# Filler products of the token norms in a two-block transformer kernel

## The reference, cut to what matters

```python
def rmsnorm(x, g):
    y = xf * rsqrt(mean(xf * xf, axis=-1, keepdims=True) + NORM_EPS)
    return y * g
# first block, per layer
h = rmsnorm(x, g_pre) * (1 + scale) + shift
x = x + gate * rmsnorm(mixer(h), g_post)
# second block, per layer
h = modulate(rms_norm(x, norm1_g), sh1, sc1)
y = conformer_conv(h, ...)     # layer 0, has a layer_norm inside
y = hgrn2_mixer(h, ...)        # layer 1
x = x + g1 * y
h = modulate(rms_norm(x, norm2_g), sh2, sc2)
x = x + g2 * sq_relu_mlp(h, w1, w2)
# at the end: rms_norm(x, final_g)
```

## The kernel before, in words

| norm | where (us of the span) | busy | followed by |
|---|---|---|---|
| post-norm and wide pre-norm, layer 0 | 346 to 368 | (2,1,3), (1,3,0) | projection of the odd mixer |
| post-norm and wide norm1, layer 1 | 702 to 725 | (2,1,3), (1,3,0) | first projection of the convolution |
| LayerNorm of the convolution | 898 to 910 | (0,2,3) | its second projection |
| norm2, layer 0 | 955 to 963 | (4,1,2) | MLP |
| norm1, layer 1 | 1318 to 1325 | (2,1,2) | projection of the recurrence |
| norm2, layer 1 | 1781 to 1790 | (4,1,2) | MLP |
| last norm | 2144 to 2155 | (2,1,0) | output |

## Time and profile before

### The profile page before, as it was taken

The page is one execution under the profiler, slowest core; times in us unless marked ns, Lnnn a source line. Parts: engine busy times, 40 slices in busy tenths (PEclk is TensorE's granted clock), DMA queues, the critical chain, the costliest instruction groups (busy, mean ns, idle before and its releaser), DMA issues.

```text
span 2157.5 us, 26466 instructions
## 1 busy us (share of the span) xinstructions
PE 2064.9 (96%) x9808; PEld 1588.1 (74%) x9808; DVE 1458.2 (68%) x2639; ACT 921.3 (43%) x1739; POOL 16.0 (1%) x15
## 2 busy tenths in 40 slices
PE   4988899999999999899999999999999899999998
PEld 2765566777667676578888887788888777888886
DVE  7667777667475799876555566998988965343343
ACT  3345554354443532344223234666666644232231
POOL 1000000000000000000000000000000000000000
PEclk8999999999999999999999999999999999999999
DMA  8522222533225111046555552111111122222321
GB/s 338 195 94 90 64 79 69 175 127 130 86 79 166 50 49 49 20 147 202 168 196 183 171 185 77 51 58 49 56 53 50 50 69 81 95 98 98 97 89 59
DMA packets 65982, 228.73 MB, mean 106 GB/s; under 512 B 7104, under 2 KB 9280, under 8 KB 65728
## 3 DMA queue, kind: packets, MB, share of 16 engines
q1 hardware_dynamic: 65856, 227.05, 31.6%
HBM read 224.93 MB, written 2.10 MB: 105 GB/s over the span
## 4 chain that ended last, share of the span: by engine, by line
PE 73%; DVE 17%; ACT 5%; issue 4%; DMA 1%; SPq 1%; DVEq 0%; ACTq 0%
PE bank L379 20%; PE bank L381 19%; PE bank L380 19%; DVE arena L1813 6%; PE bank L2099 3%; DVE w_lo L315 2%; PE bank L1259 1%; PE bank L705 1%; PE bank L1273 1%; PE bank L1284 1%; PE bank L1004 1%; DMA arena<-ada_dram 1%; ACT w_hi L306 1%; ACT arena L1302 1%; DVE arena L2045 1%
## 5 line engine op out<-in xcount | busy, mean ns | idle before, releaser
L379 PE MATMUL bank<-h_hi,w_hi 128*128 128x512 f32 x1540 | 633.2, 411 | 2.9 <-DVE h_lo L2193 0.9
L381 PE MATMUL bank<-h_hi,w_lo 128*128 128x512 f32 x1540 | 606.6, 394 | 0.0
L380 PE MATMUL bank<-h_lo,w_hi 128*128 128x512 f32 x1540 | 604.7, 393 | 0.0
L306 ACT ACTIVATE w_hi<-w_raw 128x1024 fp32r<-128x1024 f32 (+3 forms) x293 | 290.6, 993 | 282.7 <-PE bank L381 269.3
L315 DVE TENSOR_TENSOR w_lo<-w_raw,w_hi 128x1024 fp32r<-128x1024 f32 (+3 forms) x290 | 333.4, 1151 | 74.5 <-ACT w_hi L306 74.2
L379 PEld LDWEIGHTS bank<-h_hi,w_hi 128*128 128x128 f32 x1540 | 292.9, 190 | 69.1 <-issue 6.5
L381 PEld LDWEIGHTS bank<-h_hi,w_lo 128*128 128x128 f32 x1540 | 291.3, 189 | 63.9
L380 PEld LDWEIGHTS bank<-h_lo,w_hi 128*128 128x128 f32 x1540 | 292.7, 190 | 57.2 <-issue 3.9
L379 PE MATMUL bank<-a_hi_t,w_hi 128*128 128x512 f32 x512 | 203.1, 397 | 0.0
L380 PE MATMUL bank<-a_lo_t,w_hi 128*128 128x512 f32 x512 | 203.1, 397 | 0.0
L381 PE MATMUL bank<-a_hi_t,w_lo 128*128 128x512 f32 x512 | 203.0, 397 | 0.0
(11 more groups left out here) (284 smaller groups left out, 2536.8 us busy)
## 6 DMA issues: line engine op xcount, KB each, us to landing
w_raw<-weights_dram SPq DMA_DIRECT2D x261, 512.0 KB, 3.6
ada_raw<-ada_dram SPq DMA_DIRECT2D x128, 512.0 KB, 3.6
arena<-ada_dram SPq DMA_DIRECT2D x8, 1024.0 KB, 15.5
w_raw<-weights_dram SPq DMA_DIRECT2D x16, 256.0 KB, 2.6
xT<-x_dram SPq DMA_DIRECT2D x1, 2048.0 KB, 14.1
out_dram<-xT SPq DMA_DIRECT2D x8, 256.0 KB, 2.2
tables<-tables_dram SPq DMA_DIRECT2D x1, 1536.0 KB, 19.8
w_raw<-weights_dram SPq DMA_DIRECT2D x8, 144.0 KB, 3.5
```

The costliest lines, as they stand in the source:

```text
L306: nc.scalar.activation(WH[:, slot, 0:w], RAW[:, raw, 0:w], ACT.Copy).then_inc(w_hi_ready, 1)
L379: nc.tensor.matmul(o, WH[:, slot, cols], self.hi(k), start=(i == 0), stop=False)
L380: nc.tensor.matmul(o, WH[:, slot, cols], self.lo(k), start=False, stop=False)
L381: last = nc.tensor.matmul(o, WL[:, slot, cols], self.hi(k), start=False, stop=(i == self.K - 1))
```

## The change

Every `busy=...` argument of the nine `TokenNorm`s is taken out. `self.busy` is then None, so that `keep_busy` is called with a count of 0 and the wait for the filler's bank falls away. That is 45 fillers of 512 columns and 16 of 128 columns, 122 MATMUL and 122 LDWEIGHTS records. The filler products of the attention and of the recurrence are other lines of the kernel and stay.

```diff
-            post = TokenNorm(Y, C, ..., out=..., add=..., busy=(7, (2, 1, 3)))
+            post = TokenNorm(Y, C, ..., out=..., add=...)
...
-            return TokenNorm(XT, C, ..., banks=(5,), busy=(7, (1, 3, 0)), wide=True), gains
+            return TokenNorm(XT, C, ..., banks=(5,), wide=True), gains
...
-            post = TokenNorm(Y, C, ..., scratch_kb=68, busy=(7, (2, 1, 3)))
+            post = TokenNorm(Y, C, ..., scratch_kb=68)
...
-            pre, pre_gain = second_norm(0, 0, post.normed, banks=(5,), scratch_kb=68, busy=(7, (1, 3, 0)), wide=True)
+            pre, pre_gain = second_norm(0, 0, post.normed, banks=(5,), scratch_kb=68, wide=True)
...
-                norm, gains = second_norm(1, 0, p2.free, added=7, busy=(7, (2, 1, 2)))
+                norm, gains = second_norm(1, 0, p2.free, added=7)
...
-                norm = TokenNorm(XT, C, lambda k: vec("final", k), p2.free, added=7, out=..., busy=(7, (2, 1, 0)))
+                norm = TokenNorm(XT, C, lambda k: vec("final", k), p2.free, added=7, out=...)
...
-            ln = TokenNorm(Y, C, ..., func=ACT.Silu, centered=True, scratch_kb=40, banks=(6, 7), busy=(3, (0, 2, 3)))
+            ln = TokenNorm(Y, C, ..., func=ACT.Silu, centered=True, scratch_kb=40, banks=(6, 7))
...
-            n2, gains = second_norm(0, 1, pr.free, added=7, busy=(7, (4, 1, 2)))
+            n2, gains = second_norm(0, 1, pr.free, added=7)
...
-            n2, gains = second_norm(1, 1, pr.free, added=7, busy=(7, (4, 1, 2)))
+            n2, gains = second_norm(1, 1, pr.free, added=7)
```

More of the change, by code:

```diff
@@ L1525, in even_layer @@
             y2 = Project(8, 4, P, HH, HL, [], add, evac_engine="dve", chunks=mla_out.done)
-            post = TokenNorm(Y, C, lambda k: GAIN[:, 8 + k:9 + k], y2.free, added=7, out=lambda k: XT[:, k, :], add=lambda k: XT[:, k, :], busy=(7, (2, 1, 3)))
+            post = TokenNorm(Y, C, lambda k: GAIN[:, 8 + k:9 + k], y2.free, added=7, out=lambda k: XT[:, k, :], add=lambda k: XT[:, k, :])
             post_gain = gate_gain(0)
@@ L1535, in odd_norm @@
             gains = mod_gain(1)
-            return TokenNorm(XT, C, lambda k: GAIN[:, k:k + 1], made, hi=HH, lo=HL, bias=lambda k: MOD[:, 24 + k:25 + k], banks=(5,), busy=(7, (1, 3, 0)), wide=True), gains
+            return TokenNorm(XT, C, lambda k: GAIN[:, k:k + 1], made, hi=HH, lo=HL, bias=lambda k: MOD[:, 24 + k:25 + k], banks=(5,), wide=True), gains
         class HeadNorm(Stage):
@@ L1692, in odd_layer @@
                   *((Do(lambda pe, i=i: yp.chunk(pe, i, range(3))), 31.2 + 0.7 * i, 1) for i in range(C - 1)))
-            post = TokenNorm(Y, C, lambda k: GAIN[:, 8 + k:9 + k], yp.free, added=7, out=lambda k: XT[:, k, :], add=lambda k: XT[:, k, :], scratch_kb=68, busy=(7, (2, 1, 3)))
+            post = TokenNorm(Y, C, lambda k: GAIN[:, 8 + k:9 + k], yp.free, added=7, out=lambda k: XT[:, k, :], add=lambda k: XT[:, k, :], scratch_kb=68)
             post_gain = gate_gain(1)
-            pre, pre_gain = second_norm(0, 0, post.normed, banks=(5,), scratch_kb=68, busy=(7, (1, 3, 0)), wide=True)
+            pre, pre_gain = second_norm(0, 0, post.normed, banks=(5,), scratch_kb=68, wide=True)
             weave((yp, 2, 1), (ModBias(44, 48), 2.1, 1), (post_gain, 2.15, 1), (post, 3.2, 0.2, 0, 3), (post, 4.2, 1, 3, 6), (post, 6.9, 1, 6, 7), (post, 8.2, 1, 7, 8), (ModBias(48, 81), 7.2, 1), (pre_gain, 7.3, 1), (post, 8.3, 1, C, C + 1),
@@ L1753, in mlp @@
             if l == 0:
-                norm, gains = second_norm(1, 0, p2.free, added=7, busy=(7, (2, 1, 2)))
+                norm, gains = second_norm(1, 0, p2.free, added=7)
                 weave((p2, 0, 1), (ModBias(96, N_ADA), 4.1, 1), (gains, 4.2, 1), (lower_bounds(), 4.3, 1), (norm, 1.2, 1, 0, 6), (norm, 6.9, 1, 6, 7), (norm, 8.2, 1, 7, 8), (norm, 8.3, 1, 8, 9))
             else:
-                norm = TokenNorm(XT, C, lambda k: vec("final", k), p2.free, added=7, out=lambda k: XT[:, k, :], busy=(7, (2, 1, 0)))
+                norm = TokenNorm(XT, C, lambda k: vec("final", k), p2.free, added=7, out=lambda k: XT[:, k, :])
                 weave((p2, 0, 1), (norm, 1.2, 1, 0, 6), (norm, 6.9, 1, 6, 7), (norm, 8.2, 1, 7, 8), (norm, 8.3, 1, 8, 9), (norm, 9, 1, 9, 18))
@@ L1841, in conv_layer @@
             conv = DepthwiseConv(U, Y, view(56, (2, 15, P)), glu, [9] * 7 + [15])
-            ln = TokenNorm(Y, C, lambda k: vec("ln_g", k), conv.made, hi=HH, lo=HL, bias=lambda k: vec("ln_b", k), func=ACT.Silu, centered=True, scratch_kb=40, banks=(6, 7), busy=(3, (0, 2, 3)))
+            ln = TokenNorm(Y, C, lambda k: vec("ln_g", k), conv.made, hi=HH, lo=HL, bias=lambda k: vec("ln_b", k), func=ACT.Silu, centered=True, scratch_kb=40, banks=(6, 7))
             weave((n1, 0, 0.1, C + 1, 2 * C + 2), (Do(None, None, pad), 1.9, 1), (pc, 2, 1), (conv, 3.3, 1), (ln, 6.4, 2, 0, 8), (ln, 20.5, 1, 8, 9))
             pr = Project(8, C, P, HH, HL, [], residual(48 + 16), evac_engine="dve", chunks=ln.split, ada=ada_next(range(7)), outer=3, early=ln.h_ready)
-            n2, gains = second_norm(0, 1, pr.free, added=7, busy=(7, (4, 1, 2)))
+            n2, gains = second_norm(0, 1, pr.free, added=7)
             weave((ln, 0, 0.1, C + 1, 2 * C + 2), (pr, 2, 1), (n2, 3.2, 0.2, 0, 3), (n2, 4.2, 1, 3, 6), (n2, 6.9, 1, 6, 7), (n2, 8.2, 1, 7, 8), (ModBias(81, 88), 7.2, 1), (gains, 7.3, 1), (n2, 8.3, 1, 8, 9))
```

## The result

Six runs of the changed kernel have a median of 2163.69 us (2162.41 to 2169.58) against 2155.93 us (2153.83 to 2158.21): ratio 1.0039, 95% interval 1.0028 to 1.0049. It is slower, by 7.8 us between the medians, where 9.5 were forecast. The profiled execution took 2162.41 us.

What follows compares the result with a forecast made beforehand. TensorE, with 73% of the chain, was taken to bound the kernel. Losses of 18.0 us from clock falls less gains of 8.5 made it 9.5 slower: median 2155.1 to 2164.6, stated as 2164.5 us, range 2157.5 to 2171.5.

Steps and rivals of the forecast that it cites:

- The gains: In the norms, sums and spreadings no longer held back by fillers: 8.5 us saved, firm to about 1 us.
- E: Norm1 of layer 1: gain 1.0 against loss 2.6, +1.6 us; its sum was to come 0.85 earlier.
- G: The last norm: gain 1.0 against loss 0.4, -0.6 us, since only DVE and the output follow.
- F: Norm2 of layer 1: gain 2.7 against loss 2.6, -0.1 us; its sum was to come 2.55 earlier.
- D: Norm2 of layer 0: gain 1.2 against loss 3.0, +1.8 us; its sum was to come 1.05 earlier.
- A: Layer 0's post- and pre-norm: gain 0.7 against loss 2.9, +2.2 us; the post-norm's sum 0.55 earlier.
- The losses: In every norm the clock falls, slowing the next projection's start, the spreading and rarely the second sum: 18.0 us.
- The spreading's odds: Spreading at half clock, +0.9 us: charged 0.6 in both post-norms and norm2 of layer 0, 0.4 in the others.
- B: Layer 1's post- and pre-norm: gain 0.15 against loss 2.5, +2.35 us.
- The projection at half clock: Start of the projection after a norm: 4.7 us at half clock, costing 2.2 us, or 1.7 into the convolution.
- The LayerNorm: LayerNorm: gain 1.75 from an earlier spreading against loss 4.0, of which 1.8 for its slow spreading; +2.25 us.
- The pre-norms: Slow ones-products catch up before the last sum: costed at nothing, or +0.9 us in each of two if still slow.

Runs made afterwards that it cites:

- e3: Kernel before, each 512-column filler replaced by four one-column products and each 128-column filler by two: 2197.06 us, ratio 1.017.
- e4: Kernel before with the fillers out only in norm2 of layer 1: 2163.48 us, run once.
- e8: Kernel before keeping only fillers after the spreading and the pre-norms' large ones; earlier ones and the pre-norms' small ones out: 2160.52 us.
- e5: The trimmed kernel e1, but with all fillers of layer 0's post-norm back as before: 2152.32 us against 2157.75, ratio 0.9977.
- e6: As e5, also without the single filler ahead of the spreading in six norms: 2151.2 us, ratio 0.9971 against the kernel before.
- e1: Kernel before with one to three fillers fewer in five norms and the LayerNorm, the others kept: 2153.63 us against 2158.24, ratio 0.9972.
- e9: As e6, plus five fillers ahead of the LayerNorm's wait for the convolution's last chunk: 2151.89 us, ratio 0.9979 against the kernel before.

## Why the prediction was right

**The mechanism** was right: the clock falls in every norm, and the new delay is larger than what the late sums give back. e3 shows that it is the full-width fillers that held the clock, since one-column products in their places did not; e4 that it falls in a norm that alone lost its fillers, e8 the separate price at the projection, e5 and e6 that the gains are there once the clock holds. The close number (9.5 forecast, 7.8 between the medians, +8.2 in the norms) owes something to luck: the losses at the projections came out smaller than forecast (9.4 for 12.6 us), those ahead of them larger (7.3 for 5.4, if the gains were as forecast).

**The gains**, 8.5 forecast. In the changed kernel itself the second sum ends earlier after the first by 0.84 in E and G and 2.55 in F, and the LayerNorm's spreading starts 5.16 us after the sums' start instead of 6.98: 1.82 where 1.75 was forecast. With the clock held the gains measure 0.8 to 0.9 in D, E and G and 2.5 in F for the fillers taken away in e5, and 0.6 for the middle ones, where 0.9 was forecast. A's 0.55 was never seen alone, since the clock fell when one filler was taken away, and D's full 1.05 neither.

**The losses**, 18.0 forecast. If the gains were the 8.5 of the forecast, the measured +8.2 leave 16.7, and they were shared out otherwise:
- *The spreading's odds.* I gave 0.6 and 0.4 for a slow spreading. It was slow in A, B, D, E and G (1.98 to 2.08), and mostly fast in F (1.24). So G gave 0.1 instead of 0.6, and F gave 0.4 instead of 0.1. The second sum was slow in D (1.86) and in part in A (1.24). The fall came at different distances from the last dense product, 2.5 us in D and 4.5 in B, so odds were the right form, and the forecast ones were too low here.
- *The projection at half clock.* It was slow for 3.3 us in D and the LayerNorm, 3.4 in A (from 0.6 us on), 4.8 in F, 5.1 in B and 5.8 in E; the mean is 4.3, where 4.7 was forecast. What each stretch takes more behind the projection's first product is 1.4 in A, 1.1 in B, 0.7 in the LayerNorm, 1.4 in D, 2.6 in E and 2.2 in F: 9.4, where 12.6 was forecast. E cost 2.5 instead of 1.6 in full behind that start; its projection starts as far from the first sum as before (7.05 and 7.10 us), since the late sum's gain pays for the slow spreading:

```profile
1325.71 0.77 PE L397 MATMUL bank<-h_hi,w_hi 128*128 128x512 f32 x1 [1.69 <-ACT h_hi L819]
...
1331.91 0.39 PE L379 MATMUL bank<-h_hi,w_hi 128*128 128x512 f32 x1
```

- *The LayerNorm* shows best where the term was mis-sized: 2.2 forecast. Its timeline, beside the earlier trace rows:

```profile
896.50 3.58 PE L739 MATMUL bank<-tables,arena 128*128 128x1 f32 x16 [4.89 <-DVE arena L1817]
901.66 3.55 PE L776 MATMUL bank<-tables,stats 128*128 128x128 f32 x16 [1.59 <-DVE stats L852]
908.36 0.77 PE L397 MATMUL bank<-h_hi,w_hi 128*128 128x512 f32 x1 [3.14 <-ACT arena L817]
...
912.03 0.39 PE L379 MATMUL bank<-h_hi,w_hi 128*128 128x512 f32 x1
```

The spreading took 3.55 as forecast, and the projection starts 11.86 after the sums instead of 12.16. Then nine products take 3.67 us; before they took 2.68, in which 0.37 was a wait for DVE. Of the 1.0 lost, 0.3 was regained at the start and 0.3 behind, where DVE's 2.05 per chunk and TensorE's 2.07 are nearly even: +0.4 in all. I had the two numbers side by side for the convolution's first projection, and not for this one.
- *The pre-norms.* Costed at nothing, rightly: in layer 0 twelve records of ones-products take 7.96 us without a pause, the clock comes back within them, the last two wait for ACT again, and a second fall comes in the projection, after a pause of 3.14:

```profile
346.12 2.08 PE L776 MATMUL bank<-tables,stats 128*128 128x128 f32 x8 [0.57 <-DVE stats L855]
350.52 7.96 PE L760 MATMUL bank<-arena,tables 128*128 128x512 f32 x12 [2.32 <-ACT arena L792]
...
360.67 1.13 PE L760 MATMUL bank<-arena,tables 128*128 128x512 f32 x2 [0.81 <-ACT arena L792]
364.94 0.47 PE L397 MATMUL bank<-h_hi,w_hi 128*128 128x512 f32 x1 [3.14 <-ACT h_hi L819]
365.24 0.39 PE L398 MATMUL bank<-h_hi,w_lo 128*128 128x512 f32 x1
365.47 0.57 PE L397 MATMUL bank<-h_hi,w_hi 128*128 128x512 f32 x1
```

**What was missed** is layer 1's attention, -1.6 and -1.5 in the two profiles of the change. With the norms' +8.2 it gives +6.7 from the profiles, beside +7.8 between the medians (interval 6.0 to 10.6, from the ratio). And the prediction read the earlier trace rows too firmly: no pause above 2 us in the rows kept the clock, but in the profile after, one of 2.72 us did, between the same instructions.

## What to carry to other kernels

Filler products pay where they keep the clock and cost where they delay a product that is ready; the timeline tells the two apart, so trim them norm by norm (here 0.2 to 0.3% faster) and don't take them out together (0.4% slower). Fillers of 512 columns held the clock here and fillers of one column in the same places did not, and a slow clock cost most where dense work resumed. To judge a few microseconds in two thousand, compare stretches between milestones that both traces have, and not the spans.

## What the runs showed of the hardware

- A stretch that no edit touches and that stands before all edits differed by -3.8 to +0.5 us between profiles, and the attention of layer 1 by up to 6.2 us in kernels that ran the same instructions there. These stretches have falls of the clock of their own, and their number and length change from profile to profile: the pause of 2.7 us from 118 us on held a fall in the profile before and none in the profile after. That alone is nearly as large as the effect under study.
- TensorE can be busy in the trace and still lose its clock: in e3 at 974.4 us, after 3.25 us of one-column products without a pause, and in e1 at 349 us, busy to 0.97.
- Where a pause ended in a fall, filling the pause moved the fall to the next thin place (e9, the LayerNorm's spreading), and did not remove it; one profile shows it.
